# A two-layer decoder trunk: norm vectors turned on TensorE, and the order of the weight loads changed

## The reference

```python
mod = (silu(c) @ w_ada[l] + b_ada[l])
sh1, sc1, g1, sh2, sc2, g2 = jnp.split(mod, 6, axis=-1)
h = x * (1.0 + sc1) + sh1
u, q_lat, kv_lat, k_rope = jnp.split(h @ w_in[l], split_cols, axis=-1)
mixed = jnp.concatenate([pool(u), attention(q_lat, kv_lat, k_rope)], axis=-1) @ w_out[l]
x = layer_norm(ALPHA * x + g1 * mixed, ln1_g[l], ln1_b[l])
h = x * (1.0 + sc2) + sh2
ffn = shared_expert(h) + routed_experts(h)      # 64 experts, 8 for each token
x = layer_norm(ALPHA * x + g2 * ffn, ln2_g[l], ln2_b[l])
```

## Time and profile before

| | us |
|---|---|
| median of 3 runs | 1331.07 |
| lowest and highest | 1329.38, 1331.14 |
| the profiled execution | 1331.96 |
| its span in the profile | 1330.1 |

### The profile page before, as it was taken

One profiled execution on the slowest core, in us unless ns is written; L12 is line 12 of the kernel. 1 busy time (PEld: TensorE's weight loads), 2 busy tenths in 40 slices (PEclk: granted clock), 3 DMA queues, 4 the chain that ended last, 5 costly groups with the idle time before them and its releaser, 6 DMA issues.

```text
span 1330.1 us, 28125 instructions
## 1 busy us (share of the span) xinstructions
PE 1237.6 (93%) x9345; PEld 777.7 (58%) x9345; DVE 492.0 (37%) x1109; ACT 249.9 (19%) x518; POOL 158.8 (12%) x583
## 2 busy tenths in 40 slices
PE   6995999999799999999989699999998999899995
PEld 3562576666466666566646347666665666566563
DVE  5654862222122233233247337232321233222235
ACT  1223121111111111111123222111111111111113
POOL 0000012111011111111000000211110211012110
PEclk9987999999899999999989899999998999999998
DMA  9998969999999999999976953999999999999992
GB/s 322 377 406 335 374 244 422 420 420 421 421 421 421 422 421 421 398 402 387 369 284 246 395 206 112 422 389 407 421 421 421 421 421 420 420 376 390 399 407 111
DMA packets 86706, 495.90 MB, mean 373 GB/s; under 512 B 14274, under 2 KB 22482, under 8 KB 31842
## 3 DMA queue, kind: packets, MB, share of 16 engines
q1 hardware_dynamic: 86626, 494.73, 91.8%
HBM read 493.61 MB, written 1.08 MB: 372 GB/s over the span
## 4 chain that ended last, share of the span: by engine, by line
PE 86%; DMA 4%; DVE 4%; SPq 3%; issue 2%; ACT 1%; POOL 0%; DVEq 0%; POOLq 0%; ACTq 0%
PE ps L1024 31%; PE ps L1046 15%; PE ps L956 9%; PE ps L1067 8%; PE ps L966 5%; PE ps L882 4%; DMA ring<-in_w_ada 4%; PE ps L689 3%; PE ps L911 2%; SPq L500 1%; PE ps L996 1%; PE ps L1039 1%; PE ps L972 1%; PE ps L682 1%; SPq L550 1%
## 5 line engine op out<-in xcount | busy, mean ns | idle before, releaser
L1024 PE MATMUL ps<-ring,w 128*64 128x256 f32 (+1 forms) x3648 | 412.2, 384 | 0.6 <-issue 0.3
L1024 PEld LDWEIGHTS ps<-ring,w 128*64 128x64 f32 (+1 forms) x3648 | 258.5, 127 | 68.8 <-issue 14.4
L1046 PE MATMUL ps<-ring,w 128*64 128x512 f32 (+1 forms) x912 | 207.6, 597 | 0.0
L1024 PE MATMUL ps<-flex,w 128*32 128x256 f32 x736 | 169.2, 389 | 26.4 <-issue 26.3
L1024 PE MATMUL ps<-w 128*32 128x256 f32 x736 | 169.7, 390 | 0.0
L1670 DVE SCALAR_TENSOR_TENSOR w<-ps,w 128x256 f32<-128x256 f32 x57 | 27.6, 483 | 373.2 <-PE ps L1024 373.2
L956 PE MATMUL ps<-hx,scat 128*128 128x512 f32 x472 | 138.3, 417 | 0.7 <-issue 0.7
L1656 DVE CAST scat<-ps 128x512 fp32r<-128x512 f32 x114 | 78.9, 692 | 158.9 <-PE ps L1046 158.9
L1024 PEld LDWEIGHTS ps<-flex,w 128*32 128x32 f32 x736 | 80.8, 112 | 84.3 <-issue 42.1
L1204 ACT ACTIVATE w<-ps 128x512 f32<-128x512 f32 x118 | 70.6, 598 | 290.9 <-PE ps L956 290.9
L1067 PE MATMUL ps<-scat 128*128 128x512 f32 x456 | 119.2, 403 | 0.0
(11 more groups left out here) (252 smaller groups left out, 1274.1 us busy)
## 6 DMA issues: line engine op xcount, KB each, us to landing
ring<-in_w_exp_gate SPq DMA_DIRECT2D x88, 1024.0 KB, 19.5
ring<-in_w_exp_up SPq DMA_DIRECT2D x88, 1024.0 KB, 22.4
ring<-in_w_exp_down SPq DMA_DIRECT2D x88, 1024.0 KB, 22.0
ring<-in_w_ada SPq DMA_DIRECT2D x30, 1024.0 KB, 12.5
w<-in_w_exp_gate SPq DMA_DIRECT2D x20, 1024.0 KB, 16.6
w<-in_w_exp_up SPq DMA_DIRECT2D x20, 1024.0 KB, 18.9
flex<-in_w_exp_gate SPq DMA_DIRECT2D x20, 1024.0 KB, 13.8
flex<-in_w_exp_up SPq DMA_DIRECT2D x20, 1024.0 KB, 15.6
```

What stands on the lines that cost most here:

```text
L1024: last = mm(ps[unit * g:unit * g + unit, bank, 0:F], hTb[:, kt, unit * g:unit * g + unit], weights(k)[:, kt, :], start=kt == 0, stop=kt == ...
L1046: last = mm(ps[unit * g:unit * g + unit, bank, :], midT[:, f, unit * g:unit * g + unit], down_w(k)[:, f, half * 512:(half + 1) * 512], sta ...
```

## The change

- The two 4-byte loads of `ln2_g` and `ln2_b` go. Instead both are loaded at the very start as 16 rows of 512 bytes into a free part of `temp` (`gb16`), between the constants and the positions; TensorE turns them right after c, and VectorE copies the result to `colk` after it has made the rotary angles.
- `w_out` is issued in one go after the router's bias, in the place of expert 1: behind part 2's tiles 0 to 3 and in front of its tiles 4 to 7. Before, its halves stood between the tiles of parts 1 and 2.
- Expert 1 is issued after expert 0, behind the shared expert's weights.
- TensorE sums part 1 after the scores, not before them; so the scores do not wait for `gate_part`.

```diff
         c8 = temp[0:KT, 0:P]
+        gb16 = temp[0:2 * KT, P:2 * P]
...
             sp.dma_start(const[:, :], consts_dram).then_inc(s["consts_in"], 16)
+            for i, src in enumerate((ln2_g, ln2_b)):
+                sp.dma_start(gb16[i * KT:(i + 1) * KT, :], src[0:1, :].rearrange("a (k p) -> (a k) p", p=P)).then_inc(s["cols2_in"], 16)
...
-                ada_tiles(l, 1, (4, 5))
-                load_w_out(0, 4)
-                ada_tiles(l, 1, (6, 7))
-                ada_tiles(l, 2, (0,))
-                load_w_out(4, 8)
-                ada_tiles(l, 2, (1, 2, 3))
+                ada_tiles(l, 1, (4, 5, 6, 7))
+                ada_tiles(l, 2, (0, 1, 2, 3))
...
-                if l == 0:
-                    for dst, src in ((g2_col, lay(ln2_g, 0)), (b2_col, lay(ln2_b, 0))):
-                        sp.dma_start(dst, src.rearrange("a (k p) -> p (a k)", p=P)).then_inc(s["cols2_in"], 16)
                 sp.wait_ge(s["jobs_done"], (l + 1) * 12)
                 sp.dma_start(rbias, lay(router_bias, l).to_broadcast([P, E])).then_inc(s["rbias_in"], 16)
-                for half in range(2):
-                    load_gate_up(l, half, (1,), (1,))
-                load_down(l, (1,), (1,))
+                load_w_out(0, 4)
+                load_w_out(4, 8)
                 ada_tiles(l, 2, (4, 5, 6, 7))
...
                 load_down(l, (0,), (0,))
+                for half in range(2):
+                    load_gate_up(l, half, (1,), (1,))
+                load_down(l, (1,), (1,))
...
             tr(ps[:, 4, 0:KT], c8, ident[0:KT, 0:KT]).then_inc(s["cT_done"], 1)
+            pe.wait_ge(s["cols2_in"], 32)
+            tr(ps[:, 0, 0:2 * KT], gb16, ident[0:2 * KT, 0:2 * KT]).then_inc(s["gb_turned"], 1)
...
-                n = ADA_JOBS[l][1] + KT - 1
-                pe.wait_ge(ada_used[n % ADA_BUFS], n // ADA_BUFS + 2)
-                for g in range(4):
-                    last = mm(ps[32 * g:32 * g + 32, MOD_BANK[1], :], ones[:, 0:32], acc0[:, g * 512:(g + 1) * 512],
-                              start=True, stop=True)
-                last.then_inc(s["mod1_summed"], 1)
                 pe.wait_ge(s["qrT_ready"], l + 1)
...
+                n = ADA_JOBS[l][1] + KT - 1
+                pe.wait_ge(ada_used[n % ADA_BUFS], n // ADA_BUFS + 2)
+                for g in range(4):
+                    last = mm(ps[32 * g:32 * g + 32, MOD_BANK[1], :], ones[:, 0:32], acc0[:, g * 512:(g + 1) * 512],
+                              start=True, stop=True)
+                last.then_inc(s["mod1_summed"], 1)
                 modulation(l, 2, (0, 1))
...
             reduce_angle(ang, 0).then_inc(s["ang_ready"], 1)
+            dve.wait_ge(s["gb_turned"], 1)
+            v.tensor_copy(colk[:, :], ps[:, 0, 0:2 * KT])
...
-                    dve.wait_ge(s["cols2_in"], 32)
```

More of the change, by code:

```diff
@@ L368, in decoder_trunk @@
         wout_in mix_done rows1_in rows2_in ln_stats ln_std cols_in t_ready h2A_ready h2D_ready first_link gates_ready
-        table_warm back_done order_read otab_ready x1_ready x2_ready sum2_ready nmu2_ready var2_ready std2_ready part2_ready
+        table_warm back_done order_read gb_turned otab_ready x1_ready x2_ready sum2_ready nmu2_ready var2_ready std2_ready part2_ready
         h2T_done router_in rbias_in logits_done esc_ready sh_up_done R_ready shsil_ready shmid_ready sel_ready
```

## The result

| | before | after |
|---|---|---|
| median of 4 runs, us | 1331.11 | 1321.41 |
| lowest and highest | 1329.38, 1332.95 | 1319.68, 1321.91 |
| span of the profiled execution | 1330.1 | 1320.1 |

The ratio is 0.9923, 95% interval 0.9911 to 0.9935: 9.7 us faster, between 8.6 and 11.8. The forecast was 1314.3 us and its range ended at 1311.3 and 1320.0. The sign was right, the forecast gain was 7 us too large.

What follows compares the result with a forecast made beforehand. Each layer's front was bound by part 2's tile 4 landing through one in-order DMA queue, the expert stage being full. Gains 11.9+4.9=16.8 us took the profiled 1331.96 to 1315.2, the median 0.9 lower: 1314.3 us, range 1311.3 to 1320.0.

Steps and rivals of the forecast that it cites:

- Expert 1's term: Both layers' fronts: expert 1's transfer, 7.47 us per layer, no longer stands ahead of part 2's tile 4.
- From there to M3 the queue is never empty: Layer 0's front: transfers run unbroken from part 1's tile 5 to part 2's tile 3, landing at 89.2 us.
- the very value at which the prediction said it would be wrong: Sign of error: part 2's tile 3 takes over 7.5 us from issue to landing.
- the least: Lower bound, one tile still ahead of part 2's tile 3: gains 2.4 us in layer 1, 10.4 in layer 0.
- Small loads 3.75 us: Both fronts: router, rows, columns and bias take 3.75 us of queue behind part 2's tile 3, read from layer 1.
- Layer 1's cover of 2.4 us: Layer 1's front: of 9.96 us of output weight leaving the queue, 7.6 are gained; 2.4 filled idle queue and are lost.
- The cap of 12.6 us: Layer 0: VectorE's second normalising step lets TensorE gain only 0.7 us over the transfers, 12.6 at most.
- (a): Waits for part 2's tile 4: clock holds, layer 1 gains 6.6, layer 0 12.6; 1311.9 us; chance 0.14.
- (b): Layer 1's front gains nothing, uncovered idle time being 7.3 us and not 2.4; 1319.2 us; chance 0.13.
- (c): Fronts: tiles still take 12.5 us from issue to landing, losing 7.4 us per layer; 1329.1 us; chance 0.04.
- (d): Fronts: tile landings above 14.1 us make the kernel slower, 1352.1 us at 20.2; chance 0.03.
- (e): Transfers at a lower rate make expert 1 dearer, 1.3 us more per layer; 1311.7 us; chance 0.02.

Runs made afterwards that it cites:

- the halves kept: Kernel after with the two halves of the output weight put back among the tiles of parts 1 and 2: 1309.72 us, ratio 0.9843.
- the order of the sum: Kernel after with the output weight's halves back among the tiles and part 1 summed before the scores again: 1309.54 us, ratio 0.9834.
- expert 1 alone: Kernel before with expert 1 issued behind expert 0 and nothing else changed: 1314.89 us, ratio 0.9872.
- both at once: Kernel after with the output weight's halves back among the tiles and router, rows, columns and bias behind part 2's last tile: 1309.90 us, ratio 0.9834.

## Why the prediction missed

**The parts.** The sum was, in other words, 2 x 7.47 for expert 1, 4.4 for the columns and -2.4 for the output weight. The first measured 17, the second 4.4, the third -5.4, each alone; they add up to 16, close to the forecast 16.8, but the whole change gained 9.7. The first two do add: the halves kept, which is both of them together (with the sum's new place), gained 21.2. What does not add is the output weight, which cost about 11 us in their company. The step that failed is therefore its price: the prediction called it cover for nothing in layer 0 and for 2.4 us in layer 1, and the queue ran short for 3.0 and 5.6 us there (counted as time lost at 421 GB/s). Expert 1's term, 14.9, lies 2 us under what its own run gained (and inside its interval), so if anything it hid a part of the miss.

**"From there to M3 the queue is never empty", layer 0.** It runs short: 213 GB/s from 72 to 74 us. The prediction asked whether the issue keeps up for the last tile alone (M3, against its turn in the queue) and not for G6 and G7, the first two without `w_out` ahead of them. M3's issue on SyncE and its landing, of the kernel after:

```profile
84.38 0.33 SPq L428 DMA_DIRECT2D w<-in_w_ada  x1
...
88.09 2.95 SPq L538 DMA_DIRECT2D w<-in_w_out  x2
```

```profile
w<-in_w_ada SPq DMA_DIRECT2D x1, 1024.0 KB, 7.5
```

M3 lands at 91.9; 89.9 was forecast, front price included. The windows account for these 2.0 us: 1.2 are the hole from 70 to 74, and from 74 to 92 the rates (377 to 422 GB/s) lose another 0.7 against 421. M3 took 7.5 us from issue to landing, the very value at which the prediction said it would be wrong, and in layer 1 6.5 instead of 4.9. The 4.9 us of the earlier trace rows were those of a tile with only tiles near it; M3 stands behind tiles that the hole had made late. The small loads behind it are not the reason: M2, issued 2.5 us ahead of M3, took 7.5 us too, and with the small loads moved behind M7 both took 7.7. The bound called "the least" had 7.4 us for a tile and 1.5 us lost in layer 0, near what came; the forecast took the other end.

**Small loads 3.75 us.** From M3's landing to M4's, 3.75+9.96+2.49=16.2 was forecast; it took 17.8 in layer 0. The 3.75 came from layer 1 before, where the loads stood behind a full queue. Here the queue ahead of them is short, and a hole of 1.8 us opens behind. Layer 1: M3 lands at 723.27+6.5=729.8, M4 at 746.48, 16.7 us. These two points make M4 3.6 us late in layer 0 and 2.1 in layer 1.

**Layer 1's cover of 2.4 us.** The hole was foreseen near 706 and is there from 706 to 714. By rates it is 4.4 us, with 1.2 more behind the small loads. Moving the halves back shows it from the other side: 6.0 us.

**Behind M4.** The clock fell as forecast: 0.50 and 0.53, and 12.4 and 11.9 us from the landing to the projection stand near the 12.7 and 12.3 of the kernel before. The step that was off lies behind the projection. There the granted clock falls a second time in layer 0, in the kernel before as in the kernel after:

```profile
160.00:164.00 4.00, 4.00 (x27) 4.00 (x26) 2.57 (x5) 1.78 (x3) 0.00 (x0) 0.67 1.00 412
164.00:168.00 4.00, 4.00 (x19) 3.82 (x18) 3.46 (x9) 0.00 (x0) 0.00 (x0) 0.50 1.01 426
```

```profile
156.00:160.00 4.00, 4.00 (x16) 3.64 (x17) 3.97 (x8) 0.00 (x0) 0.00 (x0) 0.50 1.01 424
160.00:164.00 4.00, 4.00 (x21) 3.61 (x20) 2.66 (x3) 0.00 (x0) 0.00 (x0) 0.66 1.03 428
```

Measured from the projection's start, the fall begins about 2 us later in the kernel after, and from there to the expert stage it is 58.8 us instead of 57.8. That 1.0 and M4's 3.6, less 0.3 saved behind M4, are layer 0's missing 4.3 us. The same stretch takes 56.9 us in the halves kept, the order of the sum and expert 1 alone, where the fall is about half as long, and 57.8 us in five kernels, the one before among them. So it scatters by 1.9 us with where and how long the clock falls, and the prediction had it fixed.

**The cap of 12.6 us** in layer 0 by VectorE's second normalising step had the right mechanism and the wrong size. VectorE does set the end in both at once, but with the halves kept the stage starts 14.0 us earlier. The tiles of layer 1's part 0 that stand ahead of that step come earlier too, and in the kernel before VectorE itself waits 0.63 us for the projection just ahead of it, so the 0.7 us read there was not all of its slack. The prediction held that step fixed in time.

**Rivals.** (a), the clock holding, did not come by itself: the waits for M4 were 7.1 and 5.0 us and not some 4, and the clock fell in both; with the wait filled by matmuls it held. (b), with layer 1 gaining nothing, fell: it gained 3.2. The slower ones, (c) and (d), did not come: no tile from G7 to M3 took more than 7.5 us in the kernel after, and (c) begins above 7.6. (e) fell: from 96 to 106 us the windows of the kernel after run at 416 to 426 GB/s, and what made expert 1 worth more is mostly the time behind M4.

**The range** summed bounds of single tiles. None of its cases had the move of the output weight wrong in both layers at once, although both rest on one mechanism, the emptier queue.

## What to carry to other kernels

A load that "only fills the queue" is worth the time for which the queue behind it would run dry; count that for every tile that waits for a buffer, from the first one after the edit, and not for the last alone. Run the parts of a change one by one when they point in different directions: here the version without one of them, 1309.7 us, beats the whole one by 11.7. And price a DMA wait of TensorE with what the clock costs behind it: 7.47 us of transfer taken out of the way gave 9.4 to 9.8, though part of that lies in a stretch that scatters by 1.9 us.

## What the runs showed of the hardware

- Two loads of 1024 elements of 4 bytes each kept the queue at 51, 22 and 171 GB/s in three windows of 2 us. SyncE's 9.11 us in one issue is no fixed price: with the output weight moved behind it the same issue took 3.96.
- A hole of 1.8 us opened behind six small loads (1.3 MB) though 4 MB had been issued behind them 4 us earlier; with those loads moved, and the 4 MB issued 3.3 us sooner after M3, it was not there (111 against 414 GB/s in the same window).
- Behind a wait for DMA of 7.1 and 5.0 us, the way to the projection was 2.0 and 1.2 us longer than with 30 or 20 spare matmuls in the wait. In layer 1 only 0.4 of the 1.2 us reached the expert stage.
- In layer 0 the granted clock fell to 1.2 GHz some 31 to 34 us after the start of the projection in each of the eleven kernels whose chain shows that start, though TensorE was busy 3.49 of 4 us or more just before (kernel after: 0.98 at 152 to 156 us, 0.50 at 156 to 160). Just ahead of it, or around its start, stand 32 matmuls of one column each (3.6 to 4.8 us). No run here shows its cause.
